# The last layer's 28 input projections by seven block products in place of eight, and all of them ahead of their output products

## The chip, the cores and the metric

The kernel runs on one core of one Trainium2 chip. The time is the device time of one execution, in microseconds (us). A core has a matrix engine (TensorE, in the profile PE) and three engines for elementwise work: VectorE (DVE), ScalarE (ACT) and GpSimd (POOL). SyncE (SP) issues most DMAs. Every engine runs its own instructions in order, and engines wait for one another on semaphores. All share an on-chip memory (SBUF, 128 partitions); matmuls write into eight accumulation banks of 128 x 512 fp32 (PSUM), which the code names as four slots of two banks.

## The reference, cut to what matters

There are 1024 tokens of width 1024. A first layer (attention, a state-space branch, a convolutional feed-forward part) comes first and is not changed. Its output x2 goes into a second layer, the stage in which the change lies:

```python
h = rmsnorm(x2, norm_g)
p = h @ w_in                                   # 1024 x 1024 by 1024 x 7680
(u, v, z_a, x_b, b_g, c_g, z_b, x_c, z_c,      # 512 wide each
 g_a, g_b, g_c) = split(p)                     # the three gates 1024 wide
# v = layernorm(gelu(v)); sg = causal mix of v over blocks of 128 tokens
y_a = (gelu(u) * sg * silu(z_a)) @ w_pa        # 512 x 1024
y_b = (b_g * conv3(c_g * x_b) * silu(z_b)) @ w_pb
y_c = (pool_scale * (windows(x_c) @ w_pool) * silu(z_c)) @ w_pc
merged = sigmoid(g_a)*y_a + sigmoid(g_b)*y_b + sigmoid(g_c)*y_c
out = rmsnorm(x2 + merged @ w_o, final_g)
```

## The kernel before, in words

**Products.** An fp32 product is made of three passes, since each operand is split into a high part and the rest (low): high by high, low by high, high by low. The activations' parts are `act_h` and `act_l`. A weight block comes by DMA into `raw` (two buffers in turn), and POOL splits it in two halves: L668 copies the high part into `w_h`, L670 subtracts it and writes `w_l`. A **unit** is one block of 256 weight columns. With the whole contraction of 1024 (eight chunks of 128) and all 1024 tokens it takes 96 matmuls of 128 x 128 weights by 512 tokens; with a contraction of 512 (the products by w_pa, w_pb, w_pc, "branch products" below) it takes 48. Channels lie on partitions, so a result is a slot [128 channels, 1024 tokens].

**Order in the last stage.** v comes first: two units whose tokens lie on partitions (L1210, `rows_tile`, matmuls of 256 columns), while DVE and ACT still normalise h (L1862, L1432, L1875, eight chunks per half of the tokens). Between its matmuls lie small ones that spread statistics of x2 (L915, L922: those of the second half's norm, and a second set from `acc`, for the last rmsnorm, which DVE's `scaled_out` applies to x2 before it is stored in `x_scratch`). Then branch a: u, z_a twice; `gate_loop` with g_a and w_pa, one unit each, four times. Then branch b (x_b, c_g, b_g, z_b twice), its gate loop, branch c (x_c, z_c twice), its gate loop, and at last w_o in four units. That makes 28 input units and 12 branch products. The gates' results are read by ACT (sigmoid) straight from their slots, the branch operands stay in `in2_h` and `in2_l`, and each engine's order is written out by hand. The layer norm of v is 8 tiles of three DVE instructions (L2319, L2321, L2322) in one piece behind their statistics (L2312, L2313). The windows of x_c are a ladder of copies and adds on DVE (L2408, L2409).

**What lies between TensorE and the others.** A unit's result slots come free when ACT or DVE has read them. POOL splits a unit's weights while TensorE works at the unit before. SP loads the next block when a `raw` buffer is free (L402).

## Time and profile before

| | |
|---|---|
| median of 3 runs | 2160.37 us (2159.74 to 2160.72) |
| profiled execution | 2159.32 us, its span 2157.6 us, mean granted clock 0.996 |
| TensorE busy | 2125.6 us, 99% of the span, 10551 matmuls |
| POOL busy | 1045.3 us, 48% |
| DVE busy | 793.7 us, 37% |
| ACT busy | 412.8 us, 19% |
| chain that ended last | 94% TensorE |
| last stage | from about 1253 us (v's units) to the end; input and branch products from 1292.8 us |

The span is the time from the first to the last instruction; the execution's own time lies 1.7 us above it. "Busy" of TensorE counts modelled ends of pipelined matmuls. The chain is followed back from the last instruction to whatever released each step; a wait of TensorE shows as a piece of another engine in it. In rows of a timeline the first number is the start, the second the duration.

### The profile page before, as it was taken

How to read it: one execution, taken by the hardware profiler on the slowest of the kernel's cores; microseconds unless marked ns; L12 is line 12 of the kernel's file. 1: busy time of each engine (PE TensorE's matmuls, PEld its weight loads, DVE VectorE, ACT ScalarE, POOL GpSimd, SP SyncE). 2: the span in 40 equal slices, each digit the busy share in tenths (PEclk: the TensorE clock that was granted, in tenths of full speed). 3: DMA queues.
4: the chain of work that ended last, by engine and by line, in shares of the span. 5: the costliest groups of instructions: out<-in, count | busy, mean ns of one | idle time of the engine just before them, and what ended most of it. 6: DMA issues, size and time to landing. Idle time of an engine off the chain costs nothing.

```text
span 2157.6 us, 25639 instructions
## 1 busy us (share of the span) xinstructions
PE 2125.6 (99%) x10551; PEld 1776.3 (82%) x10551; DVE 793.7 (37%) x1093; ACT 412.8 (19%) x602; POOL 1045.3 (48%) x456
## 2 busy tenths in 40 slices
PE   6999999999999999999999999999999999999998
PEld 3888888888888888888888898888888888888878
DVE  6961355555543521222222675200031111241143
ACT  3212223232421310201111231111010110110203
POOL 2637347554453545445363545344554455536461
PEclk9999999999999999999999999999999999999999
DMA  9545554553451102011120231102111011101131
GB/s 358 130 98 162 181 166 135 156 155 127 164 203 39 49 30 78 30 49 49 32 75 30 69 134 53 39 30 68 59 40 49 30 59 58 49 30 49 49 127 79
DMA packets 149919, 192.30 MB, mean 89 GB/s; under 512 B 11112, under 2 KB 130496, under 8 KB 148800
## 3 DMA queue, kind: packets, MB, share of 16 engines
q1 hardware_dynamic: 140896, 172.06, 25.3%
q10 hardware_dynamic: 8928, 18.88, 2.3%
q8 instruction: 72, 1.18, 0.2%
q14 instruction: 23, 0.19, 0.0%
HBM read 159.21 MB, written 31.70 MB: 88 GB/s over the span
## 4 chain that ended last, share of the span: by engine, by line
PE 94%; POOL 2%; DVE 1%; DMA 1%; ACT 0%; SPq 0%; issue 0%; DVEq 0%; POOLq 0%; ACTq 0%
PE ps L747 65%; PE ps L829 8%; PE ps L777 7%; PE ps L1040 3%; PE ps L787 2%; PE ps L1001 2%; PE ps L1210 2%; POOL w_h L668 1%; DMA ada_w<-in_w_ada 1%; PE ps L1015 1%; POOL w_l L670 1%; PE ps L1281 1%; PE ps L937 0%; PE ps L1021 0%; DVE act_l L1877 0%
## 5 line engine op out<-in xcount | busy, mean ns | idle before, releaser
L668 POOL TENSOR_SCALAR w_h<-raw 128x1024 fp32r<-128x1024 f32 (+2 forms) x202 | 503.5, 2493 | 910.5 <-PE ps L747 648.3
L747 PE MATMUL ps<-act_h,w_h 128*128 128x512 f32 x1600 | 626.0, 391 | 1.5 <-POOL w_l L670 1.1
L747 PE MATMUL ps<-act_l,w_h 128*128 128x512 f32 x1600 | 623.3, 390 | 0.0
L747 PE MATMUL ps<-act_h,w_l 128*128 128x512 f32 x1600 | 623.1, 389 | 0.0
L670 POOL TENSOR_TENSOR w_l<-raw,w_h 128x1024 fp32r<-128x1024 f32 (+2 forms) x202 | 436.5, 2161 | 16.8
L747 PEld LDWEIGHTS ps<-act_h,w_h 128*128 128x128 f32 x1600 | 300.6, 188 | 68.1 <-issue 2.9
L747 PEld LDWEIGHTS ps<-act_h,w_l 128*128 128x128 f32 x1600 | 300.8, 188 | 63.0
L747 PEld LDWEIGHTS ps<-act_l,w_h 128*128 128x128 f32 x1600 | 300.8, 188 | 61.9 <-issue 0.5
L747 PE MATMUL ps<-in_h,w_h 128*128 128x512 f32 x384 | 149.9, 390 | 0.0
L747 PE MATMUL ps<-in_l,w_h 128*128 128x512 f32 x384 | 149.4, 389 | 0.0
L747 PE MATMUL ps<-in_h,w_l 128*128 128x512 f32 x384 | 149.4, 389 | 0.0
L829 PE MATMUL ps<-act_h,w_h 128*128 128x512 f32 x256 | 100.3, 392 | 0.0
L829 PE MATMUL ps<-act_l,w_h 128*128 128x512 f32 x256 | 100.1, 391 | 0.0
L829 PE MATMUL ps<-act_h,w_l 128*128 128x512 f32 x256 | 100.1, 391 | 0.0
L2199 DVE SCALAR_TENSOR_TENSOR conv<-ps,cols_b,conv 128x1023 f32<-128x1023 f32 (+1 forms) x32 | 40.8, 1282 | 140.8 <-ACT conv L1630 138.9
L2357 DVE TENSOR_TENSOR br<-br,ps 128x1024 f32<-128x1024 f32 x14 | 17.1, 1221 | 186.7 <-PE ps L747 186.7
L747 PEld LDWEIGHTS ps<-in_h,w_h 128*128 128x128 f32 x384 | 72.1, 188 | 15.1 <-issue 0.2
L747 PEld LDWEIGHTS ps<-in_l,w_h 128*128 128x128 f32 x384 | 72.1, 188 | 15.1 <-issue 0.2
L747 PEld LDWEIGHTS ps<-in_h,w_l 128*128 128x128 f32 x384 | 72.1, 188 | 15.0
L777 PE MATMUL ps<-act_h,w_h 128*128 128x512 f32 x192 | 75.9, 396 | 4.4 <-DVE act_l L1927 3.1
L693 POOL TENSOR_SCALAR k_hh<-q 128x1024 fp32r<-128x1024 f32 x8 | 22.2, 2772 | 118.1 <-DMA k_ll<-qk_scratch 118.1
L777 PE MATMUL ps<-act_l,w_h 128*128 128x512 f32 x192 | 75.2, 392 | 0.0
(363 smaller groups left out, 2868.4 us busy)
## 6 DMA issues: line engine op xcount, KB each, us to landing
raw<-in_w_in SPq DMA_DIRECT2D x45, 1024.0 KB, 5.2
raw<-in_w_up SPq DMA_DIRECT2D x16, 1024.0 KB, 5.4
ada_lo<-in_w_ada SPq DMA_DIRECT2D x16, 512.0 KB, 3.8
ada_hi<-in_w_ada SPq DMA_DIRECT2D x16, 512.0 KB, 4.8
gates_scratch<-gate_st ACTq DMA_DIRECT2D x32, 256.0 KB, 2.0
gate_in<-gates_scratch SPq DMA_DIRECT2D x16, 512.0 KB, 4.5
raw<-in_w_down SPq DMA_DIRECT2D x16, 512.0 KB, 3.4
ada_w<-in_w_ada SPq DMA_DIRECT2D x3, 2048.0 KB, 16.0
```

The source lines that it names most:

```text
L668: nc.gpsimd.tensor_scalar(w_h[:, k, c, :], src[:, c, :], 1.0, None, ALU.mult).then_inc(s["w_high"], 1)
L670: nc.gpsimd.tensor_tensor(w_l[:, k, c, :], src[:, c, :], w_h[:, k, c, :].bitcast(F32), ALU.subtract).then_inc(done, 1)
L693: stage_step(nc.gpsimd.tensor_scalar(k_hh[:, e, :], q.bitcast(F32), 1.0, None, ALU.mult))
L747: last = nc.tensor.matmul(dst[:, tok], w[:, k, kw + c, P * cg:P * cg + P], x[:, c, tok], start=(c == 0 and p == 0), stop=(c == kc - 1 and ...
L777: last = nc.tensor.matmul(slot(slots[cg])[:, tok], w[:, k, c, P * cg:P * cg + P], x[:, c, tok], start=(c == 0 and p == 0), stop=(c == kc - ...
L787: last = nc.tensor.matmul(dst[:, NB * t:NB * t + NB], x[:, c, tok], w[:, k, c, :], start=(c == 0 and p == 0), stop=(c == KD - 1 and p == 2 ...
L829: last = nc.tensor.matmul(slot(1)[:, HALF:T], w[:, n % 2, c, P * (j % 2):P * (j % 2) + P], x[:, c, tok], start=(c == 0 and p == 0), stop=( ...
L1001: last = nc.tensor.matmul(slot(t % 2)[:, c0:c0 + w], q2[:, e, P * qb:P * qb + P], k[:, e, c0:c0 + w], start=(k is k_hh), stop=(k is k_ll))
L1015: last = nc.tensor.transpose(slot(2)[:, P * b:P * b + P], src[:, P * b:P * b + P], ident[:])
L1040: last = nc.tensor.matmul(dst[:, 0:HD], src[:, P * b:P * b + P], v_st[:, pair % 2, b, HD * (h % 2):HD * (h % 2) + HD], start=(b == 0), sto ...
L1210: last = nc.tensor.matmul(rows_of(h, b, t), x[:, c, tok], w[:, 1 - b, c, :], start=(c == 0 and p == 0), stop=(c == KD - 1 and p == 2), ski ...
L2199: ins = v.scalar_tensor_tensor(conv[:, cg, j:T], slot(cg)[:, 0:T - j], cols_b[:, bass.ds(4 * q + (at_b["w_conv"] + j * (FF // P) + c), 1)] ...
```

## The change

Each of the 28 input units is cut into a 2 x 2 grid: two halves of the contraction (even and odd chunks), two halves of the unit's columns (128 each), two halves of the tokens. Where eight products of quarter blocks made up a unit, seven now do, of sums of blocks (Strassen's scheme in Winograd's form):

- **Token sums.** Once, four combinations t1 to t4 of the token quarters are formed for each of four pairs of chunks (`token_sums`): pairs 0 and 2 by POOL, pairs 1 and 3 by DVE, two adds of 1024 elements a partition, four of 512, then four subtractions of 512 for the low parts; ACT makes the high parts.
- **Weights.** For each unit POOL forms four sums of blocks (`sum1`, `sum2`, and two in place) and seven low parts `w7_l`; ACT copies the seven high parts `w7_h` (`weights_high`). All are 128 x 512. The split by L668 and L670 is gone for these units.
- **Products.** `unit(n)` on TensorE is seven calls of `seventh`, 12 matmuls of 512 each, into four banks of the unit's parity (b, a, e, d). ACT copies bank a and bank e away (`p_copied`), DVE makes the sums: `from_first` (behind the 2nd product, awaited before the 5th), `middle` (three sums behind the 5th), `last_sum` (behind the 7th). A bank is awaited by the unit after next.
- **Order.** All 28 input units come first, in the order of `UNITS`; gates go through the sigmoid to DRAM (`gates2_scratch`), branch operands to `operand_scratch`, the mixed v (`sg`) to `sg_scratch`. Then the 12 branch products run, with operands and gates loaded back, then w_o. The layer norm's normalise work is placed around units 2 and 3, the mix of v (`spatial`) ahead of units 4 to 7, the windows around units 9 and 12, the products by w_pool ahead of units 10, 11, 13, 14.
- **Statistics.** The second set of the v stage goes. x2 itself is stored, read back in eight pieces (`h_again`), squared by ACT, added by POOL (`add_square_e`) while branch products run; the small matmuls for it stand ahead of branch products 6 and 8, and DVE's scaling of x2 is at the end (`scaled_x2`, eight instructions for sixteen).

The diff, cut to its core:

```diff
+N_V2, N_S, N_P, N_WO, N_END = 55, 57, 85, 97, 101
+NS, NPRE = N_P - N_S, 7
+SLOTS = (4, 5, 6, 0, 1, 2, 3)
+UNITS = ([("gate", g, j) for g in range(2) for j in range(4)]
+         + [("xc", 0, 0), ("zc", 0, 0), ("gate", 2, 0), ("xc", 0, 1), ("zc", 0, 1), ("gate", 2, 1)]
+         + [(kind, 0, p) for p in range(2) for kind in ("u", "z")]
+         + [(kind, 0, p) for p in range(2) for kind in ("xb", "cg", "bg", "zb")]
+         + [("gate", 2, 2), ("gate", 2, 3)])
+KIND = [u[0] for u in UNITS]
+UNIT_OF = {u: n for n, u in enumerate(UNITS)}
+SG_AT, POOL_AT, WST_AT = (4, 5, 6, 7), (10, 11, 13, 14), 1
...
+            sp.wait_ge(s["prod_done"], NPRE * NS)
+            for c in range(2):
+                h_again(c)
+            for hl in range(2):
+                sp.dma_start((act_h, act_l)[hl][:, 1:KD:2, :].bitcast(F32), op_d[1, hl].rearrange("c p t -> p c t")).then_inc(op_in, 16)
+            h_again(2)
+            for m in range(2, 12):
+                load_unit(NS + m)
+                sigmoids(m)
+                if m in (2, 3):
+                    for c in range(3 if m == 2 else 6, 6 if m == 2 else KD):
+                        h_again(c)
+                if m == 7:
+                    sp.wait_ge(s["gemm"], base_p + 8)
+                    sp.wait_ge(s["sums_ready"], 5)
+                    sp.wait_ge(out_c, again(128))
+                    for hl, x in enumerate((in2_h, in2_l)):
+                        sp.dma_start(x[:].bitcast(F32), op_d[2, hl].rearrange("c p t -> p c t")).then_inc(op_in, 16)
...
+
+                pool.wait_ge(s["u_ready"], U_IN2 + KD + 2 * b + 2)
+                u0, u1 = buf[:, 0, :], buf[:, 1, :]
+                for i, u in enumerate((u0, u1)):
+                    low_step(nc.gpsimd.tensor_tensor(u, act_h[:, 2 * b + i, :].bitcast(F32), act_l[:, 2 * b + i, :].bitcast(F32), ALU.add))
+                t1, t2, t3, t4 = (tsum_f[i // 2][:, b, 2 * (i % 2) + 1, :] for i in range(4))
+                low_step(nc.gpsimd.tensor_tensor(t1, u0[:, HALF:T], u0[:, 0:HALF], ALU.subtract))
+                low_step(nc.gpsimd.tensor_tensor(t2, u1[:, HALF:T], t1, ALU.subtract))
+                pool.wait_ge(x2_out[b // 2], 16)
+                low_step(nc.gpsimd.tensor_tensor(t3, u1[:, HALF:T], u0[:, HALF:T], ALU.subtract))
+                low_step(nc.gpsimd.tensor_tensor(t4, t2, u1[:, 0:HALF], ALU.subtract))
+                for i, t in enumerate((t1, t2, t3, t4)):
+                    pool.wait_ge(s["t_high"], 4 * b + i + 1)
+                    nc.gpsimd.tensor_tensor(tsum[i // 2][:, b, 2 * (i % 2) + 1, :], t, tsum[i // 2][:, b, 2 * (i % 2), :].bitcast(F32), ALU.subtract)\
+                      .then_inc(s["tp_low"], 1)
+
+            for b in (0, 2):
+                if b:
+                    pool.wait_ge(s["tp_low"], 4)
+                    pool.wait_ge(s["u_ready"], U_IN2 + 2 * KD)
+                    pool.wait_ge(x2_out[1], 16)
+                token_sums(b, u_tmp[b])
...
+                    pool.wait_ge(s["w7_done"], NPRE * i)
+                    pool.wait_ge(s["sum_done"], 4 * i)
+                else:
+                    pool.wait_ge(s["gemm"], units_before(N_V2) + 3)
+                nc.gpsimd.tensor_tensor(sum1[:], w21, w22, ALU.add).then_inc(s["sum_done"], 1)
+                pool.wait_ge(s["sum_done"], 4 * i + 1)
+                nc.gpsimd.tensor_tensor(sum2[:], sum1[:], w11, ALU.subtract).then_inc(s["sum_done"], 1)
+                nc.gpsimd.tensor_tensor(w21, w11, w21, ALU.subtract).then_inc(s["sum_done"], 1)
+                pool.wait_ge(s["sum_done"], 4 * i + 3)
+                for o, x in enumerate((sum2[:], w11, sum1[:], w22, w21, w12, w12)):
+                    if o == 6:
+                        pool.wait_ge(s["w7_done"], NPRE * i + 6)
+                        nc.gpsimd.tensor_tensor(w12, w12, sum2[:], ALU.subtract).then_inc(s["sum_done"], 1)
+                        pool.wait_ge(s["sum_done"], 4 * i + 4)
+                    pool.wait_ge(s["w7_high"], NPRE * i + o + 1)
+                    nc.gpsimd.tensor_tensor(w7_l[:, SLOTS[o]], x, w7_h[:, SLOTS[o]].bitcast(F32), ALU.subtract)\
+                      .then_inc(s["w7_done"], 1)
+
+            for i in range(NS):
+                unit_weights(i)
+                if i == WST_AT + 1:
...
+            for m in range(12):
+                n = N_P + m
+                if m < 2:
+                    pool.wait_ge(s["prod_done"], NPRE * (NS - 1) + (5 if m else 2))
+                split(n, n % 2, 16 * (n // 2 + 1), units_before(n - 1) if m >= 2 else None, K2)
+                for c in {1: (1, 2), 2: (3, 4), 3: (5, 6), 4: (7,)}.get(m, ()):
+                    add_square_e(c)
...
             split_done(N_V2 + 1)
             for t in range(4):
                 for c in range(KD):
                     last = rows_tile(0, 1, t, c)
-                if t == 0:
-                    for th in range(2):
-                        statistics(acc, SQ_DOWN + 19, slot(1)[:, 4 * th:4 * th + 4], th)
-                if t == 2:
-                    for th in range(2):
-                        spread(6, slot(1 + th)[:, 0:HALF], diag_c[:, 4 * th:4 * th + 4])
             last.then_inc(s["gemm"], 1)
-            pe.wait_ge(s["rstd1_read"], 2)
             for c in range(KD):
                 pe.wait_ge(s["u_ready"], U_IN2 + KD + c + 1)
-                for t in range(2):
-                    rows_tile(1, 0, t, c)
+                rows_tile(1, 0, 0, c)
             for b in range(2):
-                for t in range(0 if b else 2, 4):
+                for t in range(0 if b else 1, 4):
                     for c in range(KD):
                         last = rows_tile(1, b, t, c)
                 last.then_inc(s["gemm"], 1)
...
+            def seventh(n, o, bank, high, low, first, ready=None):
+
+                pe.wait_ge(s["w7_done"], NPRE * n + o + 1)
+                for c in range(KD // 2):
+                    if ready is not None:
+                        pe.wait_ge(s["td_low" if c % 2 else "tp_low"], 4 * (c // 2) + ready)
+                    for p, (w, x) in enumerate(((w7_h, high), (w7_h, low), (w7_l, high))):
+                        last = nc.tensor.matmul(bank_of(n, bank), w[:, SLOTS[o], c, :], x(c),
+                                                start=(first and c == 0 and p == 0), stop=(c == KD // 2 - 1 and p == 2),
+                                                skip_group_check=True)
+                last.then_inc(s["prod_done"], 1)
+
...
+            def unit(n, early=0):
+
+                fresh = n < 1
+                if n < 2:
+                    pe.wait_ge(s["v2_read"], (2, 4)[n])
+                else:
+                    pe.wait_ge(s["r_done"], n - 1)
+                seventh(n, 0, "b", sums(1, 0), sums(1, 1), True, 2 if fresh else None)
+                seventh(n, 1, "a", quarter_tokens(act_h, 0, 0), quarter_tokens(act_l, 0, 0), True)
...
+                    pe.wait_ge(s["sg_read"], SG_AT.index(n) + 1)
+                if n in POOL_AT:
+                    pe.wait_ge(s["cp_ready"], 2 * POOL_AT.index(n) + 2)
+                seventh(n, 2, "e", sums(0, 0), sums(0, 1), True, 1 if fresh else None)
+                seventh(n, 3, "d", sums(3, 0), sums(3, 1), True, 4 if fresh else None)
+                pe.wait_ge(s["q_done"], n + 1)
+                seventh(n, 4, "b", sums(2, 0), sums(2, 1), False, 3 if fresh else None)
+                pe.wait_ge(s["p_copied"], 2 * n + 1)
+                seventh(n, 5, "a", quarter_tokens(act_h, 1, 0), quarter_tokens(act_l, 1, 0), False)
+                pe.wait_ge(s["p_copied"], 2 * n + 2)
+                seventh(n, 6, "e", quarter_tokens(act_h, 1, 1), quarter_tokens(act_l, 1, 1), False)
...
+            for m in range(12):
+                split_done(N_P + m)
+                if m in (0, 4, 8):
+                    pe.wait_ge(op_in, again((64, 96, 128)[m // 4]))
+                if m < 2:
+                    pe.wait_ge(s["c_done"], 3 * (NS - 1 + m))
+                    c11_out(NS - 2 + m)
+                else:
+                    pe.wait_ge(s["p_read"], 2 * (m - 1))
...
+            for n in range(NS):
+                kind, _, p = UNITS[n]
+                weights_high(n + 1, 0)
+                act.wait_ge(s["prod_done"], NPRE * n + 2)
+                if n >= 2:
+                    act.wait_ge(*released(n - 2))
+                A.activation(quad(n, 0), bank_of(n, "a"), ACT.Copy).then_inc(s["p_copied"], 1)
+                weights_high(n + 1, 1)
+                act.wait_ge(s["prod_done"], NPRE * n + 3)
+                A.activation(quad(n, 3), bank_of(n, "e"), ACT.Copy).then_inc(s["p_copied"], 1)
...
+            def from_first(n):
+
+                if n >= 2:
+                    dve.wait_ge(*released(n - 2))
+                dve.wait_ge(s["prod_done"], NPRE * n + 2)
+                dve.wait_ge(s["p_copied"], 2 * n + 1)
+                v.tensor_tensor(quad(n, 1), bank_of(n, "b"), quad(n, 0), ALU.add).then_inc(s["q_done"], 1)
...
+            def middle(n):
+
+                dve.wait_ge(s["prod_done"], NPRE * n + 5)
+                v.tensor_tensor(quad(n, 2), bank_of(n, "b"), quad(n, 0), ALU.add).then_inc(s["r_done"], 1)
+                dve.wait_ge(s["p_copied"], 2 * n + 2)
+                dve.wait_ge(s["r_done"], n + 1)
+                if KIND[n] in ("xc", "xb"):
+                    dve.wait_ge(*row_free(n))
+                v.tensor_tensor(out_of(n, 3), quad(n, 2), quad(n, 3), ALU.add).then_inc(s["c_done"], 1)
+                dve.wait_ge(s["c_done"], 3 * n + 1)
+                v.tensor_tensor(out_of(n, 2), quad(n, 2), bank_of(n, "d"), ALU.subtract).then_inc(s["c_done"], 1)
+
...
+                if before == "xc" and p == 0:
+                    windows(0)
+                if before == "xc" and p == 1:
+                    windows(2)
+                if n == 1:
+                    statistics_of(range(4))
+                if n == 2:
+                    statistics_of(range(6, QB))
+                    variance()
+                if n == 3:
+                    normalised_rows(range(2, 6))
+                middle(n)
+                if kind == "zc":
+                    windows(2 * p + 1)
+                if n == 1:
+                    statistics_of(range(4, 6))
+                if n == 2:
+                    normalised_rows(range(0, 2))
+                if n == 3:
+                    normalised_rows(range(6, QB))
+                last_sum(n)
...
-                scaled_out(th)
```

POOL, at one gate unit and one product by w_pa of branch a; `raw` is the loaded block. Before:

```order
L664 ISA [waits w_in1]
L668 TENSOR_SCALAR w_h<-raw 128x1024 [waits gemm]
L669 ISA
L670 TENSOR_TENSOR w_l<-raw,w_h 128x1024 [waits w_high]
L668 TENSOR_SCALAR w_h<-raw 128x1024
L669 REGISTER_ALU
L670 TENSOR_TENSOR w_l<-raw,w_h 128x1024 [waits w_high]
```

After, one unit (`sum_154` is `sum1`, `sum_155` is `sum2`; `w_h` and `w_l` are `w7_h` and `w7_l`):

```order
L956 TENSOR_TENSOR sum_154<-raw 128x512 [waits sum_done,w7_done,w_in0]
L958 TENSOR_TENSOR sum_155<-sum_154,raw 128x512 [waits sum_done]
L959 TENSOR_TENSOR raw<-raw 128x4x128
L967 TENSOR_TENSOR w_l<-sum_155,w_h 128x512 [waits w7_high,sum_done]
L967 TENSOR_TENSOR w_l<-raw,w_h 128x512 [waits w7_high]
L967 TENSOR_TENSOR w_l<-sum_154,w_h 128x512 [waits w7_high]
L967 TENSOR_TENSOR w_l<-raw,w_h 128x512 [waits w7_high] x3
L964 TENSOR_TENSOR raw<-raw,sum_155 128x4x128 [waits w7_done]
L967 TENSOR_TENSOR w_l<-raw,w_h 128x512 [waits w7_high,sum_done]
```

POOL's two copies and two subtractions of 1024 have become eleven additions and subtractions of 512, and seven of them wait for a copy on ACT.

DVE, at the layer norm of v (tiles of `vg`). Before, behind its statistics:

```order
L2314 TENSOR_SCALAR ln_rstd<-bn_mv 128x8 [waits dve]
L2316 RECIPROCAL ln_rstd<-ln_rstd 128x8 [waits ln_std]
L2319 TENSOR_SCALAR vg<-vg,bn_mv,ln_rstd 128x512 [waits late_in,dve]
L2321 TENSOR_TENSOR vg<-vg,ln_g 128x512 [waits dve]
L2322 TENSOR_TENSOR vg<-vg,ln_b 128x512 [waits dve]
```

After, from the third sum of unit 3 on (the triplets of L2697, L2699, L2700 stand four times ahead of this piece, too, behind `from_first` of unit 3):

```order
L2653 TENSOR_TENSOR quads<-ps,quads 128x512 [waits prod_done,dve]
L2658 TENSOR_TENSOR quads<-quads 128x512 [waits r_done,p_copied]
L2660 TENSOR_TENSOR quads<-quads,ps 128x512 [waits c_done]
L2697 TENSOR_SCALAR vg<-vg,bn_mv,ln_rstd 128x512
L2699 TENSOR_TENSOR vg<-vg,ln_g 128x512 [waits dve]
L2700 TENSOR_TENSOR vg<-vg,ln_b 128x512 [waits dve]
L2697 TENSOR_SCALAR vg<-vg,bn_mv,ln_rstd 128x512 [waits dve]
L2699 TENSOR_TENSOR vg<-vg,ln_g 128x512 [waits dve]
L2700 TENSOR_TENSOR vg<-vg,ln_b 128x512 [waits dve]
L2666 TENSOR_TENSOR quads<-ps,quads 128x512 [waits q_done,prod_done]
L2713 TENSOR_TENSOR vg<-ps,bs_row 128x8x128 [waits sg_done]
```

The normalise work stands now between sums that TensorE waits for, and the last triplet ahead of the first mix of v.

SP, at the turn to the branch products. Before, one round of a gate loop:

```order
L402 DMA raw<-in_w_in 128x8x256
L400 REGISTER_ALU
L402 REGISTER_ALU [waits w_split]
L402 DMA raw<-in_w_pa 128x4x256
```

After (`tb_f` takes x2, `x_scratch` is its store, `r_165` takes sigmoids):

```order
L718 DMA gates_scratch<-quads 256x1x512 [waits g2_sig]
L718 DMA gates_scratch<-quads 256x1x512
L789 DMA tb_f<-x_scratch 128x1024 [waits h_back0,prod_done,ada0_in1,ada0_in0]
L789 DMA tb_f<-x_scratch 128x1024
L799 DMA act_h<-operand_scratch 128x4x1024
L799 DMA act_l<-operand_scratch 128x4x1024
L789 DMA tb_f<-x_scratch 128x1024
L495 DMA raw<-in_w_pa 128x4x256 [waits w_split]
L747 DMA r_165<-gates_scratch 128x2x1024 [waits ada0_in0,sig_used]
L789 DMA tb_f<-x_scratch 128x1024 [waits hs_sq]
```

A load of branch weights, alone in its place before, now stands behind 5.5 MB of other loads, none of which was there.

## Rows read from the trace of the kernel before

**Rows 1.** The page, part 1: busy time, share of the span and instructions.
```profile
PE 2125.6 (99%) x10551; PEld 1776.3 (82%) x10551; DVE 793.7 (37%) x1093; ACT 412.8 (19%) x602; POOL 1045.3 (48%) x456
```

**Rows 2.** The chain that ended last, in time: start us, us, what.
```profile
1250.16 2.81 POOL w_l L670
...
1253.01 4.64 PE ps L1210 x24
1257.65 1.68 PE ps L915 x16
...
1265.19 1.72 PE ps L922 x4
...
1292.83 10.91 PE ps L747 x48
...
1392.99 479.38 PE ps L747 x2112
```

**Rows 3.** Busy time in windows, with PE's granted clock and DMA rate.
```profile
1250.00:1253.00 3.00, 0.20 (x1) 0.00 (x0) 2.90 (x2) 1.57 (x2) 2.87 (x2) 1.00 0.00 0
1253.00:1256.00 3.00, 2.99 (x15) 2.99 (x16) 2.86 (x3) 0.00 (x0) 0.00 (x0) 0.58 0.59 176
1256.00:1260.00 4.00, 4.00 (x33) 4.00 (x33) 3.60 (x6) 1.87 (x4) 0.00 (x0) 0.89 0.40 136
```

**Rows 4.** Timeline of POOL: a block for w_pa split, DVE idle.
```profile
1426.05 1.49 POOL L668 TENSOR_SCALAR w_h<-raw 128x512 fp32r<-128x512 f32 x1 [0.41 <-PE ps L747]
1427.63 1.28 POOL L670 TENSOR_TENSOR w_l<-raw,w_h 128x512 fp32r<-128x512 f32 x1
```

**Rows 5.** Groups of DVE (1280 to 1420 us) and ACT (1280 to 1300 us): count, busy us, mean ns.
```profile
L2319 DVE TENSOR_SCALAR vg<-vg,bn_mv,ln_rstd 128x512 f32<-128x512 f32 x8 | 6.7, 844 | 0.3
L2321 DVE TENSOR_TENSOR vg<-vg,ln_g 128x512 f32<-128x512 f32 x8 | 5.5, 692 | 0.3
...
L1696 ACT ACTIVATE vg<-ps 128x512 f32<-128x512 f32 x8 | 4.1, 605 | 9.5 <-PE ps L1210 7.2 <-DMA x_scratch<-h_t 2.3
L1696 ACT ACT_TABLE_LOAD x1 | 1.3, 1283 | 11.8 <-DVE h_t L2272 11.8
```

**Rows 6.** Timeline, DVE and POOL, at the end of branch a's gating.
```profile
1391.56 1.22 DVE L2341 TENSOR_TENSOR a_s<-a_s,a_u 128x1024 f32<-128x1024 f32 x1
1391.58 2.34 POOL L670 TENSOR_TENSOR w_l<-raw,w_h 128x512 fp32r<-128x512 f32 x1
1392.81 2.19 DVE L2343 TENSOR_TENSOR a_s<-a_s,a_z 128x1024 f32<-128x1024 f32 x1
```

**Rows 7.** Timeline, DVE and POOL, in the layer norm of v.
```profile
1301.04 2.72 DVE L2319 TENSOR_SCALAR vg<-vg,bn_mv,ln_rstd 128x512 f32<-128x512 f32 x1
1301.09 2.39 POOL L670 TENSOR_TENSOR w_l<-raw,w_h 128x1024 fp32r<-128x1024 f32 x1
```

**Rows 8.** Timeline, DVE with an operand in PSUM (`ps`) beside POOL.
```profile
1239.21 0.76 DVE L1862 SCALAR_TENSOR_TENSOR ps<-h_t,gain,ps 128x512 f32<-128x512 f32 x1
1239.25 2.41 POOL L670 TENSOR_TENSOR w_l<-raw,w_h 128x1024 fp32r<-128x1024 f32 x1
```

**Rows 9.** Timeline of DVE, then POOL, in the windows of x_c.
```profile
1901.92 2.25 DVE L2408 COPY br<-br 128x4 f32<-128x4 f32 x1
1904.21 2.02 DVE L2409 TENSOR_TENSOR br<-br 128x1020 f32<-128x1020 f32 x1
...
1900.69 3.45 POOL L670 TENSOR_TENSOR w_l<-raw,w_h 128x1024 fp32r<-128x1024 f32 x1
```

**Rows 10.** Timeline of DVE: `acc` adds, first and last of the second half's norm.
```profile
1247.37 8.00 DVE L2301 TENSOR_TENSOR acc<-acc,sq 128x1024 f32<-128x1024 f32 x4
...
1268.21 0.69 DVE L1875 TENSOR_TENSOR act_l<-sq,act_h 128x512 fp32r<-128x512 f32 x1 [0.31 <-ACT act_h L1432]
```

**Rows 11.** DMA issues at 2068 to 2072 us: count, KB each, median us to landing.
```profile
y_t<-x_scratch SPq DMA_DIRECT2D x2, 2048.0 KB, 10.9
raw<-in_w_o SPq DMA_DIRECT2D x2, 1024.0 KB, 18.5
```

971 lines of the change are left out of this document (583 added, 388 removed).

## The prediction, made before the changed kernel ran

> **What bounds the kernel now.** I read the busy shares first: TensorE 99%, POOL 48%, DVE 37%, ACT 19% [rows 1]. The chain of waits then says whether that 99% is real: in the last stage it is TensorE itself almost without a break, 2112 matmuls in 479.38 us in one piece [rows 2], a pitch of 479.38/2112 = 0.227 us, which repeats over the whole stretch. A unit of 96 is so 21.8 us, a branch product of 48 is 10.9 (10.91 stands there, [rows 2]). In this stage the other engines are covered: only one wait of size ends on TensorE, 2.8 us behind POOL's `w_l` just before 1253 [rows 2, 3]. So fewer matmuls shorten the kernel one for one, as long as what is put in their place stays covered. There lies the question, since POOL and DVE get more work per unit and deadlines inside it.
>
> **What is removed.** Twelve matmuls of each of 28 units: 336 x 0.227 = -76.3 us. A unit becomes 84 x 0.227 = 19.07 us, one seventh product 2.72. In the v stage the second set of statistics goes: 16 small matmuls 1.68 and four large 1.72 [rows 2], -3.4; and DVE's four adds to `acc` [rows 10] beside POOL's entry split, whose L670 takes 2.81 where 2.41 is usual [rows 2, 8]; the copy ahead of it is put at the same loss: -0.85. The statistics come back ahead of branch products 6 and 8, +1.7. Together -2.55; v would end at 1292.83 - 4.25 = 1288.6. Without new waits: **-78.8**.
>
> **The steady unit.** POOL has 11 instructions of 512 a unit. One subtraction of 512 alone is 1.28 us [rows 4]; with a gap of 0.09 that is 1.37, or 15.1 us, and twice a latency of ACT's copy, 16.0 us of 19.07. ACT's copy of 512 is 0.6 [rows 5]. The 5th product waits for `from_first` (`q_done`), 4 x 2.72 = 10.9 us into the unit; its two products end at 5.4, ACT's copy and DVE's sum bring it to about 8.7 (with the ACT copies ahead in the queue): slack 2.2. A gate unit costs no wait so, as long as nobody is in POOL's way.
>
> Whether somebody is, is the disputed price. When a DVE instruction with both inputs in SBUF meets POOL's subtraction, the two take turns: POOL's 512 takes 2.34 in place of 1.28, and DVE's multiply right behind 2.19 in place of 1.22 [rows 6]; a DVE TENSOR_SCALAR of 512 took 2.72 until POOL's 2.39 was over, the other seven (6.7 - 2.72)/7 = 0.57 [rows 5, 7]; a copy of four columns took 2.25 and POOL 3.45 where 2.4 is usual [rows 9]. With an operand in PSUM nobody waits: 0.76 and 2.41 at the same moment [rows 8]. Of the five sums in a unit four read PSUM and one (the second of `middle`, 0.69) doesn't: steady gate units stay clean. The branch work and the norm don't: there it is SBUF by SBUF. The bounds are then each engine's own time, and the sum of both.
>
> The Trainium skill, page "SBUF — State Buffer", section "Who interferes with whom", states this as a lock: a DVE instruction with two SBUF inputs, or one in a two-port mode, and a GpSimd instruction that reads SBUF exclude each other for a whole instruction, and one with a PSUM operand is free. The trace agrees (2.34 for 1.28, [rows 6]). By this rule every SBUF-only overlap below costs its full length, which is the upper bound of each term.
>
> **The waits that the change adds.**
>
> *Entry of unit 0.* TensorE needs the token sums. POOL forms pair 0 from 1252.1 on (after the v split), pair 2 behind it: each 2 x 2.4 + 8 x 1.28 = 15.1, so done at 1283.3 with gaps. DVE's pairs 1 and 3 start when the norm ends: at 1268.9 in the trace, now some 5.8 earlier, as the adds to `acc` end at 1255.4 [rows 10] where the norm's statistics would let it begin at about 1250.8, and a diagonal of 1.22 goes too. So from 1263.1, 4 x 1.22 + 16 x 0.69 = 15.9. ACT's gelu of v stands behind both, four tiles and a table load 4 x 0.6 + 1.3 = 3.7 [rows 5], a weight copy 0.6, POOL's low part 1.28: 1288.9 to 1289.5, a wait of up to 0.9. If POOL and DVE take turns, 20.2 + 15.9 us lie behind 1263.1: 1299.2, ACT and POOL 5.6 more, and the wait is 16.2, with gaps 17. All of DVE's part is SBUF by SBUF: nearer to turns, **13**.
>
> *Unit 0.* ACT's first weight copy of unit 1 reads POOL's sum of unit 1, which POOL begins only after unit 0's eleven; ACT's copy of bank a stands behind it. `from_first(0)` comes so at about 15.8 for 10.9: **5** (4 to 6).
>
> *Unit 4.* The mix of v waits for all normalised tiles. Behind `from_first(3)` (8.7 into unit 3) stand six tiles of 0.57 + 2 x 0.69 and gaps, 2.04 each, and `middle` 2.1: 8.7 + 14.4 = 23.1 for 19.07, a wait of 4.1 alone. With turns between 18 SBUF instructions and POOL's up to 15: the sums of unit 3 come late too, and ACT's copies behind them hold POOL. **12**.
>
> *Units 10 and 13.* The windows (ladders of 1024, 1.2 an instruction, [rows 9]) stand between `middle` and `last_sum` of unit 9 and around unit 12, where the products by w_pool and their bank wait: 0 to 5 and 2 to 12; **11.5** together.
>
> *Units with gating (z, u, c_g, b_g, z_b).* Four to six SBUF multiplies of 512, 0.69 each, ahead of `from_first` against its slack of 2.2: 0 to 5.5; **2**.
>
> *Branch products.* At their start SP issues 1 MB of x2, 4 MB of operands and 0.5 MB of x2 ahead of the weights of product 2. Loads are served in turn: w_o's 1 MB landed 18.5 us after issue behind 4 MB, which landed after 10.9 at the median [rows 11]. At 0.27 to 0.3 MB a us the third piece of x2 lands about 20 us in; its square on ACT 1.06 (estimated from 0.6 for half the width), POOL's add 2.4, then the split 2 x (1.49 + 1.28) [rows 4], as POOL does them in that order: 29.5 for 21.8, **8** (5 to 12). Before product 8 the same again, its weights behind 4 MB: **3** (0 to 4).
>
> *The clock.* After the wait of 2.8 us before 1253 the granted clock was 0.58 for 3 us, then 0.89 for 4 [rows 3]: 3 x 0.42 + 4 x 0.11 = 1.7 us lost at the return. Seven waits of that size or above are listed: bounds 3 (two) to 11, **8**.
>
> **The sum.** 13 + 5 + 12 + 11.5 + 2 + 11 + 8 = 62.5 us of waits against -78.8: -16.3. The profiled execution took 2159.32 (span 2157.6 and 1.7 around it); the forecast for it is 2143.0. The median of the runs lies 1.05 above it, so **2144**.
>
> **The rivals.**
> - *The cover holds* (0.22): engines meet rarely, only the uncontended waits stay: 0.9 + 5 + 4.1 + 2 + 11 + 5 = 28, -50.8, **2110**. For it: POOL is 48% busy and DVE 37% now [rows 1], and most overlaps of the trace cost nothing. Against: in the changed stage POOL would be at 80% (15.1 of 19.07), so that nearly every SBUF instruction of DVE meets one of its.
> - *Turns everywhere* (0.22), the other side: the port is the bound at entry, layer norm and windows. The upper bounds: 17 + 6 + 16 + 17 + 5.5 + 16 + 11 = 88.5, +9.7, **2170**. It decides as soon as the waits pass 78.8, that is if each turn costs both engines as in rows 6. The skill's lock, taken for every overlap, gives this case.
> - *POOL is the bound of the unit* (0.06): it reads with a stride now (every other chunk, half the columns) and writes in place; if an instruction takes 1.7 in place of 1.28 us, the unit is 11 x 1.79 + 0.9 = 20.6 for 19.07, and 28 x 1.5 = 42 us come on top: **2187**. It decides above 1.56 us. No row shows a strided read of POOL.
> - *Nothing changes* (0.08): gains and waits cancel, 2156 to 2165.
> - My forecast holds 0.42, with its own range of 2124 to 2156.
>
> **How the numbers follow.** About 0.2% (4.3 us) is what a measurement of this kernel can tell from no change. Faster: 0.42 + 0.22 = 0.64; same 0.08; slower 0.22 + 0.06 = 0.28. The range goes from the lower rival (2110) to where the upper one and half of the last are inside, 2182; outside remain a cover better than the first rival's and a POOL far slower, some 0.15. The low bounds of all terms would give 2100, the high ones 2170.
>
> **What the profile after would show.** The removed part: 3 x 4 x 7 = 84 matmuls a unit at 0.227 and units at 19.1 us over the eight gates at the start; more than that at a pitch of POOL's eleven is the third rival. The disputed price: the waits of TensorE on `tp_low`, `td_low` at about 1289 (16 us: turns; 1 us: cover), on `vn_ready` ahead of unit 4, on the windows' results ahead of units 10 and 13, on the weights of branch product 2. DVE's subtractions in token sums at 0.69 would mean cover, at 1.5 to 2 turns. The forecast is wrong if waits arise at places that I priced at nothing: the write-back of gates (a unit's bank and quads come free by a DMA of the unit two before), the loads of a unit's weights (1 MB in the 19 us), or POOL waiting for ACT's copies while ACT waits for TensorE, which would turn 16.0 us of a unit into more than 19.07.

## The result

| | before | after |
|---|---|---|
| median | 2158.97 us (2156.60 to 2161.88, 9 runs) | 2166.85 us (2164.03 to 2167.91, 9 runs) |
| ratio, 95% interval | 1 | 1.0035 (1.0025 to 1.0045) |
| span of the profiled execution, mean clock | 2157.6 us, 0.996 | 2165.8 us, 0.98 |

The changed kernel is 0.35% slower, 7.6 us of 2159. I forecast 2144 and faster with 0.64; the value lies inside my range and next to the rival that I called turns everywhere (2170), but that nearness is luck, as the account below shows. One execution of experiment 7 took 9774 us at full clock; it is left out of that ratio, and no trace shows what it was. TensorE's busy time, the first line of the page after, fell by 52.5 us against [rows 1], with 336 matmuls fewer, and the span still grew:

```profile
PE 2073.1 (96%) x10215; PEld 1722.8 (80%) x10215; DVE 972.9 (45%) x1258; ACT 559.8 (26%) x902; POOL 1235.8 (57%) x679
```

The waits of TensorE behind other engines, from 1240 us on (engine, line, whom it waited for: us in all, times, longest):

```profile
PE ps L1517 <- ACT vg L1989: 15.4, 1, 15.4
PE ps L1582 <- DVE vg L2700: 13.4, 1, 13.4
PE ps L1614 <- POOL w_l L855: 12.5, 1, 12.5
PE ps L1517 <- issue: 9.2, 2, 7.0
PE ps L1517 <- DVE quads L2641: 3.9, 3, 2.5
PE ps L1183 <- POOL w_l L855: 3.8, 1, 3.8
PE ps L1471 <- POOL w_l L868: 2.4, 1, 2.4
PE ps L1592 <- DVE r L2732: 2.1, 1, 2.1
PE ps L1038 <- POOL w_l L855: 1.6, 1, 1.6
```

That is 60.3 us in the places that I had named (all rows but two that the kernel before had too: L1471, there 2.8 us on L1210, and L1038 of w_o, there 1.3): the entry of unit 0 (15.4), unit 4 (13.4, the mix of v), branch product 2 (12.5), units 10 and 13 (9.2 + 2.1: of the two waits marked "issue", 7.0 us stand in unit 13 and 2.2 in unit 10), unit 0 and the gated units (3.9 together, 2.5 in unit 0) and branch product 8 (3.8). Behind each of the long ones the clock was at its lower level, 1.2 GHz, when TensorE was back. Three windows just behind such waits (busy of the engines, then PEclk):

```profile
1403.00:1406.20 3.20, 3.20 (x19) 3.20 (x20) 0.49 (x1) 0.63 (x1) 1.02 (x1) 0.51 0.63 222
...
1306.80:1310.50 3.70, 3.70 (x9) 2.93 (x10) 0.00 (x0) 2.86 (x6) 3.70 (x4) 0.50 0.02 4
1940.10:1945.40 5.30, 5.29 (x13) 4.14 (x14) 0.00 (x0) 0.00 (x0) 5.15 (x3) 0.50 0.57 208
```

TensorE is busy throughout, at half the full clock, where in [rows 3] the return from a shorter wait took 0.58 for 3 us. All stretches at half clock in which TensorE was busy add up to 24.2 us here, so 12.1 us were lost by them; one of 3.4 us (1.7 lost) stands in the v stage of both kernels and is not in this sum.

**At the entry**, the timeline of POOL, DVE and ACT shows the token sums and what stands behind them:

```profile
1281.10 1.62 POOL L928 TENSOR_TENSOR tb_f<-u_tmp 128x512 f32<-128x512 f32 x1
1284.51 2.15 POOL L931 TENSOR_TENSOR tb_f<-u_tmp 128x512 f32<-128x512 f32 x1
```

```profile
1287.78 1.68 DVE L2618 TENSOR_TENSOR tb_f<-u_tmp 128x512 f32<-128x512 f32 x1
...
1299.44 1.75 DVE L2625 TENSOR_TENSOR tb<-tb_f,tb 128x512 fp32r<-128x512 f32 x1
```

```profile
1301.25 1.28 ACT L1989 ACT_TABLE_LOAD   x1 [6.08 <-DVE tb L2625]
1302.54 2.07 ACT L1989 ACTIVATE vg<-ps 128x512 f32<-128x512 f32 x4
```

POOL's instruction of 512, 1.28 alone [rows 4], takes 1.6 to 2.15, DVE's 0.69 [rows 5] takes 1.68 to 1.75: the two engines take turns, all the way from 1264 to 1301.2. Then come the table load, four gelu tiles, the first weight copy and POOL's first low part, as the chain of the prediction had it, and TensorE starts at 1306.8.

**Unit 4.** DVE's normalise work, behind `from_first` of unit 3, and POOL at the end of it:

```profile
1380.34 0.54 DVE L2697 TENSOR_SCALAR vg<-vg,bn_mv,ln_rstd 128x512 f32<-128x512 f32 x1
1380.91 1.67 DVE L2699 TENSOR_TENSOR vg<-vg,ln_g 128x512 f32<-128x512 f32 x1
...
1398.19 1.37 DVE L2697 TENSOR_SCALAR vg<-vg,bn_mv,ln_rstd 128x512 f32<-128x512 f32 x1
1401.25 1.63 DVE L2700 TENSOR_TENSOR vg<-vg,ln_b 128x512 f32<-128x512 f32 x1
```

```profile
1397.56 1.71 POOL L967 TENSOR_TENSOR w_l<-raw,w_h 128x512 fp32r<-128x512 f32 x1 [6.87 <-ACT w_h L2006]
```

Where TENSOR_SCALAR meets POOL it takes 1.37 us for 0.54, the multiply and the add behind it 1.63 to 1.67 for 0.69. Nine of the eighteen instructions behind `from_first` do so, which adds 8.3 us to DVE's work here. POOL in turn waited 6.87 us for a weight copy that stood on ACT behind `middle` of unit 3.

**Unit 13**, DVE at the end of the ladders of window 2 and of window 3 (the chains of copies and shifted adds that form the window sums), where 16-wide instructions take 1.1 us:

```profile
1598.61 1.11 DVE L2732 TENSOR_TENSOR r<-r 128x16 f32<-128x16 f32 x1
...
1609.53 1.12 DVE L2730 TENSOR_TENSOR r<-r,inv 128x16 f32<-128x16 f32 x1
```

**Branch product 2**, the chain that ended last (start, us, what):

```profile
1906.48 0.64 ACT quads L2035
...
1907.69 4.13 DMA gates_scratch<-quads
...
1911.88 0.34 SPq L789
...
1913.78 17.17 DMA tb_f<-x_scratch
...
1934.41 1.50 POOL w_h L853
```

The last sigmoid's store to DRAM (4.13 us) stands ahead of the reads of x2, since SP waits for it; so the first read is issued 6.3 us into product 0, and the third read lands 17.17 us after its issue, behind 5 MB. The weights of product 2, issued right behind it at 1914.46, took 18.0 us to land, so they were there at 1932.4; POOL's add of squares, which stands ahead of their split, ran until 1934.4. Of the 12.5 us some 2 are so the order on POOL and the rest the queue.

**The steady unit** has no wait. This is the chain over the last two units and the last three products of the one before:

```profile
1858.66 47.07 PE ps L1517 x204
```

47.07 / 204 = 0.2307 us a matmul, against 0.227 in [rows 2]. From start to start a unit takes 19.25 us (1867.05 to 1886.30) where I took 19.07. The trace shows where the rest lies, here in the last unit, at the end of its 3rd product and in its 5th:

```profile
1893.56 0.39 PE L1517 MATMUL ps<-tb,w_l 128*128 128x512 f32 x1
1894.23 0.39 PE L1517 MATMUL ps<-tb,w_l 128*128 128x512 f32 x1
...
1898.44 0.40 PE L1517 MATMUL ps<-tb,w_l 128*128 128x512 f32 x1
1899.14 0.40 PE L1517 MATMUL ps<-tb,w_l 128*128 128x512 f32 x1
```

From one matmul to the third behind it are 0.67 us in the 3rd product and 0.70 in the 5th. From the first matmul of the 4th product (1894.46) to the ninth of the 6th (1901.93) lie 32 pitches of 0.233 us on average; all others are 0.227. The seven products so take 2.72, 2.72, 2.72, 2.82, 2.80, 2.76 and 2.72 us from start to start, the same in every unit without a wait, also in the traces of experiments 1, 9, 10, 11 and 12. It is no wait, and the cause is open.

POOL's low parts that read `raw` with a stride (line, shapes, count, busy us, mean ns), beside units 7 and 8, are not slower for it; those that read a sum without one took 1295 ns there:

```profile
L967 POOL TENSOR_TENSOR w_l<-raw,w_h 128x512 fp32r<-128x512 f32 x7 | 9.1, 1293 | 6.2 <-ACT w_h L2006 6.2
```

### The profile page after: what moved, and what is told of

It is laid out like the page before. It is cut to its first block and busy times, and to the rows that moved or that the text cites. A ratio compares the mean times of both kernels' runs of the same rounds, so it can differ in the third digit from the quotient of the medians.

```text
span 2165.8 us, 25830 instructions
## 1 busy us (share of the span) xinstructions
PE 2073.1 (96%) x10215; PEld 1722.8 (80%) x10215; DVE 972.9 (45%) x1258; ACT 559.8 (26%) x902; POOL 1235.8 (57%) x679
## 5 line engine op out<-in xcount | busy, mean ns | idle before, releaser
L1517 PE MATMUL ps<-tb,w_h 128*128 128x512 f32 x896 | 285.6, 400 | 28.5 <-ACT vg L1989 15.4
L1008 PE MATMUL ps<-act_h,w_h 128*128 128x512 f32 x704 | 276.8, 393 | 1.4 <-POOL w_l L855 1.0
L1008 PE MATMUL ps<-act_l,w_h 128*128 128x512 f32 x704 | 274.9, 390 | 0.0
L1008 PE MATMUL ps<-act_h,w_l 128*128 128x512 f32 x704 | 274.7, 390 | 0.0
L967 POOL TENSOR_TENSOR w_l<-raw,w_h 128x512 fp32r<-128x512 f32 x140 | 197.2, 1413 | 90.2 <-ACT w_h L2006 90.0
L1517 PEld LDWEIGHTS ps<-tb,w_h 128*128 128x128 f32 x896 | 170.1, 191 | 71.8 <-issue 28.7
L1517 PE MATMUL ps<-tb,w_l 128*128 128x512 f32 x448 | 178.2, 398 | 0.0
L1008 PEld LDWEIGHTS ps<-act_h,w_h 128*128 128x128 f32 x704 | 132.7, 188 | 30.8 <-POOL w_l L855 2.0
L1008 PEld LDWEIGHTS ps<-act_l,w_h 128*128 128x128 f32 x704 | 132.8, 189 | 27.8 <-issue 0.5
L1008 PEld LDWEIGHTS ps<-act_h,w_l 128*128 128x128 f32 x704 | 132.7, 189 | 27.7
L1517 PE MATMUL ps<-act_l,w_h 128*128 128x512 f32 x336 | 131.3, 391 | 0.0
L1517 PE MATMUL ps<-act_h,w_h 128*128 128x512 f32 x336 | 131.2, 390 | 0.0
L1517 PE MATMUL ps<-act_h,w_l 128*128 128x512 f32 x336 | 130.7, 389 | 0.0
L1090 PE MATMUL ps<-act_h,w_h 128*128 128x512 f32 x256 | 100.3, 392 | 0.0
L1090 PE MATMUL ps<-act_l,w_h 128*128 128x512 f32 x256 | 100.1, 391 | 0.0
L1090 PE MATMUL ps<-act_h,w_l 128*128 128x512 f32 x256 | 100.1, 391 | 0.0
```

The lines of the kernel that those rows point to most:

```text
L967: nc.gpsimd.tensor_tensor(w7_l[:, SLOTS[o]], x, w7_h[:, SLOTS[o]].bitcast(F32), ALU.subtract)\
L1008: last = nc.tensor.matmul(dst[:, tok], w[:, k, kw + c, P * cg:P * cg + P], x[:, c, tok], start=(c == 0 and p == 0), stop=(c == kc - 1 and ...
L1090: last = nc.tensor.matmul(slot(1)[:, HALF:T], w[:, n % 2, c, P * (j % 2):P * (j % 2) + P], x[:, c, tok], start=(c == 0 and p == 0), stop=( ...
L1517: last = nc.tensor.matmul(bank_of(n, bank), w[:, SLOTS[o], c, :], x(c), start=(first and c == 0 and p == 0), stop=(c == KD // 2 - 1 and p ...
```

## The experiments

Ratios are to the kernel before, measured on the same chip, with their 95% interval. The changed kernel itself stands at 1.0035; differences to it are ratio differences times 2159 us, good to some 3 us. A single wait repeats from trace to trace to about 1 us: the one at branch product 2, 12.5 us in the changed kernel's trace, is 11.3 to 11.6 in six others that leave it as it was.

### 1. Eight products again

```diff
+                for c in range(KD // 2 if o == 1 else 0):
+                    for p, (w, x) in enumerate(((w7_h, high), (w7_h, low), (w7_l, high))):
+                        last = nc.tensor.matmul(bank_of(n, bank), ..., start=(c == 0 and p == 0), ...)
```

> The changed kernel with the second product of every unit computed twice (the same 12 matmuls again, the same result), so that a unit has 96 matmuls as before. Theory 1 (the seven products are worth what they remove, and the loss lies in waits at a few places, which more matmuls elsewhere don't cover): 28 x 2.72 = 76 us longer than the changed kernel, less what the longer unit absorbs at units 1, 4 and 13, some 5 to 10, so +66 to +76, and some 75 to 84 us above the kernel before. Rival (TensorE was held back in every unit by POOL or ACT, so that removed matmuls were worth little): +10 to +40 only, since the added matmuls would fill idle time.

Measured: 2220.68 us, 1.0287 (1.0271 to 1.0302), +54 us to the changed kernel. Its waits:

```profile
PE ps L1587 <- DVE vg L2705: 11.0, 1, 11.0
PE ps L1619 <- POOL w_l L855: 10.3, 1, 10.3
PE ps L1517 <- issue: 4.8, 1, 4.8
```

Steady units take 21.97 us, exactly 2.72 more than 19.25: the removed product is worth what it removes. But the longer units absorb more than I expected, 11.0 for 13.4, 4.8 for 9.2 + 2.1, nothing for 3.9, 10.3 for 12.5; with the clock behind them that is some 18 us in the traces, and 22 of 76 by the ratios. The total, +54, lies between Theory 1 (+66 to +76) and the rival (+10 to +40) and would not decide by itself; the 2.72 us in every steady unit do, and by them the rival falls, while Theory 1 holds in kind and misses in size. And all that came with the scheme, its waits, the reorder and the sums, costs 1.0287, 62 us, when nothing is saved.

### 2. The mix of v one unit later

```diff
-SG_AT, POOL_AT, WST_AT = (4, 5, 6, 7), (10, 11, 13, 14), 1
+SG_AT, POOL_AT, WST_AT = (5, 6, 7, 8), (10, 11, 13, 14), 1
```

> The mix of v stands one unit later (ahead of units 5, 6, 7, 8 in place of 4, 5, 6, 7), nothing else is changed. Theory 1 (the 13.4 us ahead of unit 4 are a deadline set too early for the normalise work on DVE): that wait goes; in its place from_first of unit 4 comes some 3 us late, so 10 us of waiting and 1 to 2 us of slower clock are won, -9 to -12 against the changed kernel. Rival (DVE is behind for good there, because POOL's turns slow it): the wait moves to unit 5 or to the 5th product of unit 4 with nearly its full length, 0 to -4.

Measured: 2160.02 us, 1.0000 (0.9991 to 1.0009), -7.6 us. The row of 13.4 is gone; what is late next is `from_first` of unit 4, and it has grown from 3.9 in three waits:

```profile
PE ps L1517 <- DVE quads L2641: 9.3, 4, 5.7
```

5.7 us stand there, not 3. The result lies between the two theories, nearer to the first: some 8 us were the early deadline, and 5 to 6 us of DVE's work, turns included, are carried into the next unit.

### 3. Weights ahead of the other loads

```diff
             base_p = units_before(N_P)
+            load_unit(NS + 2)
...
-                for c in {1: (1, 2), 2: (3, 4), 3: (5, 6), 4: (7,)}.get(m, ()):
+                for c in {3: (1, 2), 4: (3, 4), 5: (5, 6, 7)}.get(m, ()):
```

On SP the later reads of x2 move from products 2 and 3 to 4 and 5, and the operand loads of branch c behind the weights of product 8.

> Order on the SP queue and on POOL alone: the weights of branch product 2 are loaded ahead of the reads of x2 and the operands, those of product 8 ahead of its operands, and POOL adds the squares of x2 two products later. Theory 1 (the waits of 12.5 and 3.8 us are loads queued behind 5.5 and 4 MB): both go, with the slow clock after them, -17 to -20 us. Rival (the operands of product 4, or the squares, are late next, or the queue is full anyway): -0 to -8, with a new wait ahead of product 4, 6 or 8.

Measured: 2155.23 us, 0.9979 (0.9970 to 0.9989), -12 us. Products 2 and 8 start in time. But:

```profile
PE ps L1635 <- POOL w_l L859: 3.8, 1, 3.8
...
PE ps L1618 <- POOL w_l L859: 2.3, 1, 2.3
```

The 2.3 us stand ahead of product 3, whose weights now land 16.26 us after their issue behind the same loads. The 3.8 us stand ahead of product 6, here on the timeline of TensorE:

```profile
1975.78 3.57 PE L1635 MATMUL ps<-ones,tb_f 128*128 128x1 f32 x16 [3.76 <-POOL w_l L859]
```

I had put three adds of squares ahead of POOL's split for product 6; that split is late by 3.8 us, and the sixteen small matmuls behind it take 3.57 us, at half clock, where the same sixteen take 1.68 in [rows 2]. So both waits went, as Theory 1 said, and a part of the win went into two new ones, the kind that the rival named; -12 lies between the two. The run changed the order on SP and on POOL at once and doesn't part them; the landing time in the changed kernel's trace (above) does, and gives most of it to the queue.

### 4. Token sums without turns

```diff
-                sum_step(v.tensor_tensor(t1, u0[:, HALF:T], u0[:, 0:HALF], ALU.subtract))
+                sum_step(v.tensor_tensor(t1, u0[:, HALF:T], other[:, 0:HALF], ALU.subtract))
```

`other` is slot 0 in PSUM, and so in all ten instructions of a pair on DVE. One wait is new, for the unit of v that fills this slot.

> DVE's token sums take their second operand from a PSUM bank (its contents at that time, so the sums of pairs 1 and 3 are other numbers and the output is not the reference's); count, order and size of the instructions are as before. Theory 1 (turns with POOL at the shared access to SBUF make the wait at entry): DVE's 512 instructions take 0.7 and not 1.67 us, POOL's 1.3 and not 1.7, the token sums are done by about 1286 us in place of 1301, and the wait of 15.4 us falls to 0 to 3: -12 to -16 us against the changed kernel. Rival (the engines' own work is too long, turns or not): DVE 0.7 but POOL as slow as now, the wait stays above 8, -0 to -7.

Measured: 2153.74 us, 0.9974 (0.9964 to 0.9985), -13 us. The timeline, POOL and DVE at the same time, and the wait at entry:

```profile
1277.63 1.30 POOL L931 TENSOR_TENSOR tb_f<-u_tmp 128x512 f32<-128x512 f32 x1
```

```profile
1276.87 0.69 DVE L2620 TENSOR_TENSOR tb_f<-u_tmp,ps 128x512 f32<-128x512 f32 x1
```

```profile
PE ps L1517 <- ACT vg L1989: 2.3, 1, 2.3
```

0.69 and 1.30 side by side, and 2.3 us of 15.4 are left. The instructions are the same in number, order and size, only an operand's place differs: the turns made 13 us of this wait. The Trainium skill's rule (page "SBUF — State Buffer", section "Who interferes with whom") says just this, that a DVE instruction with at most one input in SBUF, outside the two-port modes, doesn't contend with GpSimd; the trace agrees, with 0.69 and 1.30 at the same time. Unit 0, which TensorE now starts some 13 us earlier, waits 4.3 us for `from_first` in place of 2.5, near the 5 that I had forecast for it.

### 5 and 6. Three pairs on DVE; then ACT's work ahead of the last sums

```diff
-            for b in (0, 2):
...
-                token_sums(b, u_tmp[b])
+            token_sums(0, u_tmp[0])
...
-            for b in (1, 3):
+            for b in (1, 2, 3):
```

The second kernel also takes `value_rows(0, t)` and `weights_high(0, 0)` to `(0, 2)` on ACT ahead of `token_high(3)`.

> POOL forms the token sums of pair 0 alone and DVE those of pairs 1, 2 and 3, in place of two and two; nothing else is changed and the result is the same numbers. Theory 1 (turns at the shared access to SBUF): what counts is the sum of both engines' work behind the norm, and DVE's 8.2 us a pair replace POOL's 15.1; the sums end at about 1295 us and not 1301, the wait at entry falls from 15.4 to 9 to 11, -4 to -7 us. Rival (each engine at its own pace, POOL's sums the bound): DVE's three pairs, 24.6 us from 1264 on, would be the bound at 1289, and the wait would fall to 2 to 4, -11 to -14.

> As the one before, and ACT takes the gelu of v's first half of the tokens and the first weight copies ahead of the last token sums, where they waited behind all of them. Theory 1 (behind the last sum stood 5.6 us of ACT's and POOL's work that needs none of it): a further 4 to 6 us, -9 to -12 against the changed kernel. Rival (the first product then waits for the second half's gelu or the banks): -4 to -7, as the one before.

Measured: 2160.99 us, 1.0006 (0.9997 to 1.0015), -6 us, and 2158.33 us, 0.9992 (0.9984 to 1.0001), -9 us. The wait at entry in the one and in the other:

```profile
PE ps L1512 <- ACT vg L1984: 10.9, 1, 10.9
```

```profile
PE ps L1512 <- DVE tb L2630: 5.0, 1, 5.0
```

10.9 is what the sum of both engines' work gives, and far from the 2 to 4 of the rival. The second kernel wins 5.9 us more at the entry and only 3 by the ratios: in its trace unit 0 waits 4.4 us and not 2.5, and TensorE works for 5.8 us at half clock behind that. With turns, an instruction belongs where it is shorter: DVE's pair is 8.2 us, POOL's 15.1.

### 7. The ladders of the windows in DVE's gap

```diff
+                if before == "xc":
+                    windows(2 * p, 0)
                 from_first(n)
```

> The first steps of the ladders of windows 0 and 2 stand ahead of from_first of units 9 and 12, where DVE was idle for 8 us, and not behind it. Theory 1 (the waits of 2.1 and 7.0 us at unit 13 and 2.2 at unit 10 are DVE's ladders queued into its second half of the unit): 3 to 7 us of them go, and with them a part of the slow clock at unit 13, -4 to -9 us. Rival (the ladders delay from_first and so the 5th product): the waits move to units 9 and 12, -1 to +3.

Measured: 2160.98 us, 1.0001 (0.9992 to 1.0010), -7 us. The waits of 2.2 and 2.1 us are gone, the third stays (7.0 before), so its trace shows 3.5 us less of waits in these units; that is less than the 7 of the ratios, but not more than their 3 us off:

```profile
PE ps L1517 <- issue: 7.8, 1, 7.8
```

### 8. All of it together

The edits of 2, 6 and 7; the normalise work spread (two tiles ahead of `from_first` of units 3 and 4, one behind it); ACT's copy of bank a ahead of unit 1's first weight copy in unit 0; branch products as in 3, with one or two adds a product:

```diff
+            for c in {2: (1,), 3: (2, 3), 4: (4, 5), 5: (6, 7)}.get(m, ()):
```

> All reorderings together, the arithmetic unchanged: the entry of the kernel above, the mix of v one unit later with its normalise work spread over idle stretches of DVE in units 3 and 4, the windows as above, the copy of bank a ahead of unit 1's first weight copy in unit 0, and branch products with the weights first and POOL's adds of squares one or two a product. Theory 1 (the seven products give what they remove, the loss is in waits at six places and the clock behind them): 60 us of waits and 12 of slow clock shrink to some 15 to 25 in all, -42 to -55 against the changed kernel, so 1.6 to 2.2% faster than the kernel before. Rival (waits move on to the next place, as the mix of v did in part): -20 to -35.

Measured: 2123.55 us, **0.9833 (0.9820 to 0.9845)**, -44 us to the changed kernel, inside Theory 1. Its two longest waits stand at units 13 and 3:

```profile
PE ps L1515 <- issue: 7.8, 1, 7.8
PE ps L1515 <- DVE quads L2652: 6.9, 4, 5.4
```

### 9. The last ladder later

```diff
+                temps = [ladder[:, i, :] for i in range(2)] if c == 3 else [r3[:, 2 + i, :] for i in range(2)]
...
-                if kind == "zc":
-                    windows(2 * p + 1)
+                if kind == "zc" and p == 0:
+                    windows(1)
...
+                if n == 13:
+                    windows(3, 0)
```

> The combined kernel with the largest ladder (window 3) moved behind the read-out of the product by w_pool in unit 13, its two temporary rows in a place that is free by then, and one tile of v's norm less ahead of from_first in units 3 and 4. Theory 1 (the 7.8 us at unit 13 are DVE busy with a ladder whose result is needed only a unit later, the 7.7 of unit 3 two tiles too many in a gap of 8 us): both go but for 1 to 3 us, -9 to -15 us against the combined kernel. Rival (DVE and POOL turns carry it over): the wait stands at unit 13's 5th product or ahead of unit 14 with most of its length, 0 to -5.

Measured: 2113.05 us (2110.76 to 2113.46), **0.9778 (0.9764 to 0.9791)**, -12 us to the combined kernel, inside Theory 1, and 48 us under the kernel before. The longest waits that are left:

```profile
PE ps L1516 <- DVE tb L2637: 5.0, 1, 5.0
PE ps L1613 <- POOL w_l L859: 2.5, 1, 2.5
PE ps L1516 <- DVE quads L2653: 2.4, 4, 0.7
```

### 10. TensorE kept busy through two waits

```diff
+                if n == 4:
+                    extra_free(n)
+                    for i in range(56):
+                        nc.tensor.matmul(extra_of(n)[:, 0:HALF], act_h[:, 1, 0:P], act_h[:, 1, 0:HALF], start=True, stop=True)
```

and 52 likewise ahead of branch product 2, on the changed kernel.

> The changed kernel, with 56 more matmuls into an unused bank while TensorE waits ahead of unit 4, and 52 while it waits for the weights of branch product 2 (their results are overwritten; the output is as before). Theory 1 (a wait costs its own length, and then the clock at half speed for 3 to 5 us of work, because the engine was idle): the granted clock stays full through both places, the two rows of wait shrink to 0 to 2 us, and the time falls by what the slow clock took there, 1.6 + 2.7 = 4 us (3 to 5). Rival (the slow clock comes from something else than the idle time, such as the load of all engines): it stays or gets worse, and the time is 0 to +4.

Measured: 2161.37 us, 1.0006 (0.9997 to 1.0015), -6 us. The filling at unit 4, and the clock behind it:

```profile
1384.93 12.86 PE L1579 MATMUL ps<-act_h 128*128 128x512 f32 x56
```

```profile
1398.00:1406.00 8.00, 7.38 (x50) 6.48 (x51) 2.38 (x3) 1.26 (x2) 1.87 (x3) 1.00 0.79 266
```

The granted clock stays at 1.00 where the changed kernel had 0.51 for 3.2 us. The two stretches behind unit 4 and product 2 are gone (half of 3.2 + 5.3, so 4.3 us), the one at entry, left idle, is there as before. So the slow clock comes with the idle time, and matmuls whose results nobody reads earned 4 us by the trace and 6 by the ratios.

### 11. No adding onto a closed bank

```diff
-start=(first and c == 0 and p == 0)
+start=(c == 0 and p == 0)
```

> The changed kernel with the 5th, 6th and 7th product of each unit started anew in their banks in place of added to what the first three left there (so the unit's output lacks those three products); count and waits are as before. A steady unit takes 19.25 us where 84 matmuls at 0.227 are 19.06, and the starts of the 5th, 6th and 7th product are 0.05 to 0.08 late. Theory A (adding onto a closed bank costs it): units of 19.06, some 5 us less in all. Theory B (the extra wait for another engine ahead of these three costs it, though it has long come): units stay at 19.25.

One execution: 2167.04 us. The steady stretch of the chain:

```profile
1858.65 47.06 PE ps L1517 x204
```

Unchanged, and product by product the same 2.82, 2.80 and 2.76: Theory A falls. Theory B falls by the same traces, and so does what I had built both on: the 5th, 6th and 7th product start late only because the matmuls ahead of them, in the 4th, the 5th and the first nine of the 6th, come 0.233 us apart. The 4th product has no second wait, and the 7th, which has one, runs at 0.227. It isn't the work on the next unit's weights either, since the last unit has no next one and shows the same pitch. What these 33 matmuls have that others lack was not tried.

### 12. Eight products in the combined kernel

The edit of experiment 1 on the kernel of experiment 8.

> The combined kernel with the second product of each unit computed twice, so with 96 matmuls a unit as before. Theory 1 (with the waits away, a removed product is worth its 2.72 us): 28 x 2.72 = 76 us longer than the combined kernel, less 8 to 14 that the longer unit absorbs at units 0, 3 and 13: +62 to +70, so 1.2 to 1.5% above the kernel before. Rival (what the combination won was cover by other means, and POOL's unit is close to TensorE's): +35 to +55.

Measured: 2182.93 us, 1.0105 (1.0090 to 1.0121), 59 us above the combined kernel. Its waits where the combined kernel had 7.8 and 6.9:

```profile
PE ps L1515 <- issue: 3.0, 1, 3.0
PE ps L1515 <- DVE quads L2657: 1.8, 1, 1.8
```

That is a little under the expectation of +62 to +70 and above the rival's +55: the longer unit absorbs 17 us here by the ratios, of waits and clock. With the order mended, the scheme's bill is 1.05%, 23 us, and no longer 62; the seven products then earn 59.

## Why the prediction was wrong

The step that failed is **the sum**, not the mechanism: "13 + 5 + 12 + 11.5 + 2 + 11 + 8 = 62.5 us of waits against -78.8" left a margin of 16.3, and the runs showed 72.4 us of waits and clock, 2.0 more for the statistics, and 7.4 in two terms that I had put at nothing. Every place that I had named was a wait, and no wait stood where I had priced nothing. The terms that were most off are the branch products (11, measured 16.3), the pitch inside the units (0, measured 5.3) and the clock (8, measured 12.1).

| step | forecast | measured | |
|---|---|---|---|
| twelve matmuls of 28 units | -76.3 | -76.3 | 2.72 a product in every steady unit, experiment 1 |
| v stage | -4.25 | -4.25 | v ended at 1291.1 in a trace that stood 2.5 us later; 1292.83 - 4.25 + 2.5 |
| statistics back | +1.7 | +3.7 | 1.7 ahead of product 6, and ahead of product 8 3.63 with 1.65 of slow clock in it, so 2.0: I had counted the sixteen small matmuls and not the four large |
| entry | 13 | 15.4 | turns, experiments 4 to 6 |
| unit 0 | 5 | 2.5 | TensorE's late start gave POOL time: 4.3 and 4.4 where it starts earlier, experiments 4 and 6 |
| unit 4 | 12 | 13.4 | experiment 2 |
| units 10 and 13 | 11.5 | 11.3 | experiments 7 and 9 |
| gated units | 2 | 1.4 | |
| branch products | 11 | 16.3 | experiment 3; some 15.2 with product 2 as in the other traces |
| clock | 8 | 12.1 | experiment 10 |
| inside the units | 0 | 5.3 | 28 x 0.19, cause open, experiment 11 |
| mix of v and w_pool | 0 | +2.1 | 4 x 3.48 + 4 x 1.76 = 21.0 for 2 x 5.99 + 2 x 3.43 = 18.8 |

The measured terms give -80.55 + 3.7 + 72.4 + 5.3 + 2.1 = +2.95. The trace after stands 2.5 us later than the one before from the 600th matmul on (137.01 for 134.49 us), ahead of anything that the change touches; other traces here stand from 1.9 us earlier to 2.4 later, so that is chance of this pair and no cost. With it and 0.9 at w_o and the tail, 6.4 of the span's 8.2 us are placed, and 2 are not.

**Branch products** were the largest miss in a single term. The step read "at their start SP issues 1 MB of x2": I let the issue begin with the product. It began 6.3 us later, behind the last gate's sigmoid and its store of 4.13 us, which SP waits for. The rate, and the order on POOL, were right. A second piece of this term is product 8, 3.8 us for 3.

**The clock**: I priced 1.7 us a wait from one wait of 2.8 us [rows 3] and then took 8 of bounds of 3 to 11. The long waits cost 1.6 to 2.7 each and unit 13, with its two waits in a row, 4.3: the true sum lies above my upper bound.

**Entry and unit 4**: the mechanism and the upper bounds (17, 16) were right, and "nearer to turns" should have been taken at its word: by turns alone POOL and DVE end at 1299.2, and they ended at 1301.2 in a trace that stood 2.5 us later. The lock of the Trainium skill (page "SBUF — State Buffer", section "Who interferes with whom"), taken at its full length, gave this number, and I took less. At unit 4 turns made 8.3 us of DVE's lateness, and 4.1 had been forecast without any: together 12.4 of the 13.4.

**The margin**: my own range for the likeliest case went to 2156, and the terms' upper ends made 2170. With a net of 16 out of two numbers near 70, the sign was a coin's toss, and 0.64 for faster said more than the rows bore. Of the 24.5 us between the span that I forecast (16.3 shorter) and the span measured (8.2 longer), 9.9 are terms of waits and clock that I had priced too low on balance, 9.4 are terms priced at nothing or half, 2.5 are chance, and the rest is 0.9 at the tail and what isn't placed.

Of the rivals, the bound of POOL's unit falls by its row (1.29 us strided, as contiguous); that the cover holds falls by the entry. Turns everywhere gave 2170, and 2167 was measured, but by luck: its waits and clock were to be 88.5 us and are 72.4, and the rest came from terms that it had at nothing. Turns did happen at entry, in unit 4 and in the windows, and in the gated units too, but there `from_first` had slack enough that TensorE waited 1.4 us and not 5.5 (four multiplies of 512 on L2672 at 1673.34 take 4.81 us, and 2.8 alone).

## What to carry to other kernels

When a change trades many matmuls against new work on the helpers, look for the places where a deadline stands inside a stage, and ask for each whether the same work could stand a stage later: here a handful of reorderings, and one pair of sums given from GpSimd to VectorE, with the same arithmetic, turned 0.35% slower into 2.2% faster. Where VectorE and GpSimd both work out of SBUF, plan with the sum of their times, give each instruction to the one on which it is shorter, or put one operand into PSUM. And where the gain is the difference of two large sums, let the chances say so.

## What the runs showed that I had not expected

- A turn can cost a small instruction as much as a large one: DVE's 16-wide steps of the ladders took 1.11 to 1.15 us beside POOL, and 0.17 alone.
- Matmuls whose results nobody reads, issued in place of an idle wait, kept the granted clock at 1.00 and made the kernel 4 to 6 us shorter.
- In each unit 33 matmuls in a row, from the first of the 4th product to the ninth of the 6th, come 0.233 us apart and not 0.227, 0.19 us a unit, with nothing to wait for, and not because they add to a closed bank. The cause is open.
